# Weight remainders moved from GpSimd to the Vector engine, roundings moved behind the norms, and half of the sums of squares moved ahead

## The reference

```
mod = silu(c) @ w_ada + b_ada                      # six shift/scale/gate vectors
h = modulate(rmsnorm(x)); same for the context
u, q, k, v, z, beta, g = mixer_inputs(h)           # h @ w_in, short convolutions, l2norm of q and k
o = bidirectional gated delta rule, chunks of 64 (here 128 tokens each)
y = concat(fourier(u), rmsnorm(o) * silu(z)) @ w_out
x += gt1 * rmsnorm(y)
x += gt2 * rmsnorm((silu(conv3x3(gate)) * val) @ w_down),  val, gate = modulate(rmsnorm(x)) @ w_up
layer A: x += (bgate * conv3(cgate * h)) @ w_out_a,  bgate, cgate, h = rmsnorm(x) @ w_in_a
layer B: x += (gelu(y) * (rglru forward + backward)(conv4(u))) @ w_out_b,  y, u = rmsnorm(x) @ w_in_b
after A and after B:  x += mixture of 32 experts, top 2 (rmsnorm(x));  x += sigmoid(rmsnorm(x) @ w_ple_gate + b) * (p @ w_ple)
out = rmsnorm(x)
```

## Time and profile before

| | us |
|---|---|
| median of 3 runs (1904.95 to 1909.45) | 1907.88 |
| the profiled execution, its time | 1911.88 |
| its span, first to last instruction | 1910.1 |
| busy: PE / DVE / ACT / POOL | 1692.1 / 717.3 / 506.2 / 452.3 |
| mean granted TensorE clock | 0.944 |

### The profile page before, as it was taken

The page is one execution under the profiler, slowest core; times in us unless marked ns, Lnnn a source line. Parts: engine busy times, 40 slices in busy tenths (PEclk is TensorE's granted clock), DMA queues, the critical chain, the costliest instruction groups (busy, mean ns, idle before and its releaser), DMA issues.

```text
span 1910.1 us, 25856 instructions
## 1 busy us (share of the span) xinstructions
PE 1692.1 (89%) x10638; PEld 1148.1 (60%) x10638; DVE 717.3 (38%) x1312; ACT 506.2 (27%) x772; POOL 452.3 (24%) x211
## 2 busy tenths in 40 slices
PE   5988886999979779999999998894799999999987
PEld 2677686999969744443443446793644444444447
DVE  1447534899257531221221213537412212212223
ACT  3434343444433111111111105346211111111123
POOL 2336324587438210000000004461100000000011
PEclk9999887999989879999999998897899999999999
DMA  9122442343636529999999993332569999999970
GB/s 407 59 108 85 181 188 89 133 177 127 213 118 250 223 100 390 429 428 428 428 428 429 428 428 155 145 132 100 253 254 429 428 428 428 428 429 429 429 296 23
DMA packets 37510, 527.99 MB, mean 276 GB/s; under 512 B 4160, under 2 KB 4288, under 8 KB 4800
## 3 DMA queue, kind: packets, MB, share of 16 engines
q1 hardware_dynamic: 36864, 525.22, 66.7%
q10 hardware_dynamic: 576, 1.75, 0.3%
HBM read 525.91 MB, written 1.05 MB: 276 GB/s over the span
## 4 chain that ended last, share of the span: by engine, by line
PE 51%; DMA 32%; DVE 10%; ACT 5%; issue 1%; POOL 0%; SPq 0%; DVEq 0%; ACTq 0%
DMA ring<-in_w_up 30%; PE bank L469 23%; PE bank L933 14%; PE bank L534 2%; PE bank L959 2%; DMA ring<-in_dense 2%; PE bank L462 2%; ACT ring_rounded L1077 1%; PE bank L889 1%; DVE hT L1595 1%; PE bank L890 1%; PE bank L639 1%; ACT L1107 1%; DVE xn L1582 1%; DVE work L1654 1%
## 5 line engine op out<-in xcount | busy, mean ns | idle before, releaser
L1463 POOL TENSOR_TENSOR ring_rounded<-ring,ring_rounded 128x2048 fp32r<-128x2048 f32 (+1 forms) x81 | 362.0, 4490 | 405.4 <-ACT ring_rounded L1077 405.4
L933 PE MATMUL bank<-ring,work 128*64 128x512 f32 x1536 | 342.6, 600 | 35.5 <-DMA ring<-in_w_up 33.4
L469 PE MATMUL bank<-xn_rounded,ring_rounded 128*128 128x256 f32 (+1 forms) x2560 | 355.6, 292 | 14.3 <-DVE xn_rounded L1569 14.2
L469 PEld LDWEIGHTS bank<-xn_rounded,ring_rounded 128*128 128x128 f32 x2560 | 330.6, 197 | 21.1 <-issue 17.1
L933 PEld LDWEIGHTS bank<-ring,work 128*64 128x64 f32 x1536 | 109.5, 138 | 264.5 <-issue 208.2
L469 PE MATMUL bank<-work_rounded,ring_rounded 128*128 128x256 f32 (+1 forms) x1424 | 221.1, 301 | 46.7 <-POOL work_rounded L1540 26.9
L1533 POOL TENSOR_TENSOR work<-work_rounded,work 128x128 f32<-128x128 f32 x64 | 24.3, 401 | 863.5 <-PE bank L952 854.0
L469 PEld LDWEIGHTS bank<-work_rounded,ring_rounded 128*128 128x128 f32 x1424 | 194.0, 197 | 57.4 <-issue 27.8
L959 PE MATMUL bank<-ring,work 128*64 128x512 f32 x1024 | 226.8, 595 | 0.0
L2018 DVE TENSOR_TENSOR work<-work,bank 128x512 f32<-128x512 f32 x32 | 22.0, 688 | 429.2 <-PE bank L933 429.2
L1077 ACT ACTIVATE ring_rounded<-ring 128x2048 fp32r<-128x2048 f32 (+1 forms) x88 | 154.7, 1808 | 63.8 <-PE bank L469 43.4
(11 more groups left out here) (304 smaller groups left out, 1726.5 us busy)
## 6 DMA issues: line engine op xcount, KB each, us to landing
ring<-in_w_up SPq DMA_DIRECT2D x64, 2048.0 KB, 17.3
ring<-in_w_down SPq DMA_DIRECT2D x64, 2048.0 KB, 13.2
ring<-in_dense SPq DMA_DIRECT2D x50, 2048.0 KB, 8.0
work<-in_w_gate SPq DMA_DIRECT2D x32, 2048.0 KB, 21.8
ring<-in_w_gate SPq DMA_DIRECT2D x32, 2048.0 KB, 21.5
ring<-in_dense SPq DMA_DIRECT2D x8, 1408.0 KB, 6.2
ring<-in_dense SPq DMA_DIRECT2D x2, 1024.0 KB, 14.5
work<-in_ctx SPq DMA_DIRECT2D x1, 1024.0 KB, 6.6
```

Source lines behind the costliest of these rows:

```text
L469: last = mm(out, rv(ring[r][:, at:at + P]), rv(x[part][k]), start=k == 0 and j == 0, stop=k == n_k - 1 and j == 2)
L933: last = mm(b[64 * y:64 * y + 64, :], xg[:, k, 64 * y:64 * y + 64], ws[y][:, 512 * k:512 * k + 512], start=k == 0, stop=k == KT - 1)
L1463: pool.tensor_tensor(rv(w), w, rv(ring[HIGH_SLOT[n]][:, a:b]), ALU.subtract).then_inc(S["w_low"], 1)
```

## The change

1. `BY_DVE` is gone; `by_dve` in `plan` is now a set of (chunk, half). DVE makes both halves of `w_in` chunks 3 and 4, `w_out` 1, `w_up` 1, `w_in_a` 1 to 5, `w_out_a` 0 and 1, `ple0` 1, `w_in_b` 0 to 3, `w_out_b` 0 and 1, `ple1` 1, and the seven halves of before: 45 of 88. It does so in a new helper, `weights_low`, called at set places in its stream.
2. ACT's `split_next` moves: in the front behind the gates' exponential (`w_in` 4); behind the `cat` tiles (`w_out` 1); behind `scaled_input` instead of before the squares (`w_up` 1, `w_in_a` 1); behind the last `yT` tile (`w_out_a` 1); behind the norm of layer B (`w_in_b` 1).
3. `sum_squares` can be called in two parts. In `w_out`, `down`, `out_a` and `out_b` the first four tiles are summed before the projection's last use.
4. In z and u the six sums of squares of q and k come two behind each of the first three uses, none behind the last; ACT copies the second u bank after all six roots.

```diff
-    by_dve = [first["w_down"] + c for c in range(2, 8)] + [first["w_in_a"]]
+    by_dve = [(first[name] + c, half) for name, chunks in (
+        ("w_in", (3, 4)), ("w_out", (1,)), ("w_up", (1,)), ("w_in_a", range(1, 6)), ("w_out_a", range(2)), ("ple0", (1,)),
+        ("w_in_b", range(4)), ("w_out_b", range(2)), ("ple1", (1,))) for c in chunks for half in range(2)]
+    by_dve += [(first["w_down"] + c, 0) for c in range(2, 8)] + [(first["w_in_a"], 0)]
...
             for b in range(2, uses):
+                if summed and b == uses - 1:
+                    sum_squares(early)
                 dense_split(*tiles(b), x)
...
-                    first = {"z": 0, "u": 3}[stage] + 2 * b
-                    for a in range(first, min(first + 2 - b * (stage == "z"), 6)):
+                    for a in {("z", 0): (0, 1), ("z", 1): (2, 3), ("u", 0): (4, 5)}.get((stage, b), ()):
                         sums_qk(a)
...
-        projection("w_out", "w_out", 4, [...], ("cat_ready", 1))
+        projection("w_out", "w_out", 4, [...], ("cat_ready", 1), True)
-        sum_squares()
+        sum_squares(late)
         ready = norm_input()
         projection("up", "w_up", FT, xparts, ready)
         for b in range(4):
+            if b == 3:
+                sum_squares(early)
             dense_split(USE["down"] + b, ...)
...
@scalar
-        split_next()                       # behind the q SiLUs
         act.wait_ge(S["ab_dve"], 1)
...
         signal(act.activation(gtmp[1], gtmp[1], ACT.Exp, scale=-1.0), "ab_act")
+        split_next()
...
-        split_next()                       # behind the roots of o
         for h in range(HEADS):
             act.wait_ge(S["cat_gated"], h + 1)
             high(cath[:, 4 + h], cat[:, 4 + h])
+        split_next()
...
             root(bank[4][:, 0:SEQ], bank[5][:, 0:SEQ], 1.0 / D, "ss_ready", "rstd_ready")
-            split_next()                   # end of rows
...
         scaled_input(24)
+        split_next()
...
         scaled_input()                     # before in_a
+        split_next()
-            if j in (1, 2, 3, 5, 6, 7):
+            if j in (1, 2, 3, 5, 6):
                 split_next()
...
         high(yh[:, 6:8], yT[:, 6:8])
+        split_next()
...
-                if layer == 0 and b % 2:
+                if layer == 0 and b == 1:
                     split_next()
...
         scaled_input()                     # before in_b
+        split_next()
@vector
+        def weights_low(n, halves=(0, 1)):
+            for half in halves:
+                a, b = parts_of(n)[half]
+                dve.wait_ge(S["w_high"], 2 * SPLITS.index(n) + half + 1)
+                w = ring[SLOT[n]][:, a:b]
+                count["w_low_dve"] = count.get("w_low_dve", 0) + 1
+                v.tensor_tensor(rv(w), w, rv(ring[HIGH_SLOT[n]][:, a:b]), ALU.subtract).then_inc(S["w_low_dve"], 1)
...
             free(ins, n)                   # q convolutions, b = 0, 1
+            weights_low(FIRST["w_in"] + 3, (b,))
...
                "gates_ready")
+        weights_low(FIRST["w_in"] + 4)
...
             low(cat[:, 4 + h], cath[:, 4 + h], "cat_ready")
+        weights_low(FIRST["w_out"] + 1)
         residual(lambda k: gains[:, 3, k:k + 1])
         scaled(hT, lambda k: gains[:, 2, k:k + 1])
+        weights_low(FIRST["w_up"] + 1)
...
         scaled(hT, lambda k: par("norm_mix", k, 1))
+        weights_low(FIRST["w_in_a"] + 1)
...
+            if j in (1, 2, 3, 5):
+                weights_low(FIRST["w_in_a"] + (1, 2, 3, 5).index(j) + 2)
+            elif j == 6:
+                weights_low(FIRST["w_out_a"])
         low_pair(6)
+        weights_low(FIRST["w_out_a"] + 1)
...
             scaled(hT, lambda k: par("norm_ple", 8 * layer + k, 1))
+            weights_low(FIRST[f"ple{layer}"] + 1)
...
+                if layer == 0 and b == 1:
+                    weights_low(FIRST["w_in_b"])
...
         scaled(hT, lambda k: par("norm_mix", 8 + k, 1))
+        weights_low(FIRST["w_in_b"] + 1)
...
             free(last, n)                  # conv4 of layer B, uses b = 0..3
+            if b % 2:
+                weights_low(FIRST["w_in_b"] + 2 + b // 2)
+        weights_low(FIRST["w_out_b"])
...
                 last = v.tensor_tensor(gi[d][:, j], gi[d][:, j], uu[:, j], ALU.mult)
+                if d == 0 and j == KT // 2:
+                    weights_low(FIRST["w_out_b"] + 1)
```

More of the change, by code:

```diff
@@ L163, in plan @@
         for half in range(2):
-            name = "w_low_dve" if n in by_dve and half == 0 else "w_low"
+            name = "w_low_dve" if (n, half) in by_dve else "w_low"
             made[name] += 1
             low_done[n, half] = (name, made[name])
-    return first, use, free, slot, arrival, load_after, splits, high_slot, high_after, by_dve, low_done
-FIRST, USE, FREE, SLOT, ARRIVAL, LOAD_AFTER, SPLITS, HIGH_SLOT, HIGH_AFTER, BY_DVE, LOW_DONE = plan()
+    return first, use, free, slot, arrival, load_after, splits, high_slot, high_after, low_done
+FIRST, USE, FREE, SLOT, ARRIVAL, LOAD_AFTER, SPLITS, HIGH_SLOT, HIGH_AFTER, LOW_DONE = plan()
 WORK, WORK_N = layout([
@@ L517, in first_uses, with projection @@
                     assert signal(last, "dense_full") == use + 1
-        def projection(stage, chunk, uses, x, ready):
+        early, late = range(4), range(4, KT)
+        def projection(stage, chunk, uses, x, ready, summed=False):
             def tiles(b):
@@ L525, in projection, with sum_squares @@
             for b in range(2, uses):
+                if summed and b == uses - 1:
+                    sum_squares(early)
                 dense_split(*tiles(b), x)
-        def sum_squares():
-            for k in range(KT):
+        def sum_squares(tiles=range(KT)):
+            for k in tiles:
                 if k % 2 == 0:
@@ L534, in sum_squares @@
                 last = mm(bank[4][:, 0:SEQ], ones, sq1[:, k], start=k == 0, stop=k == KT - 1)
-            signal(last, "ss_ready")
-            count["norms"] = count.get("norms", 0) + 1
+            if tiles[-1] == KT - 1:
+                signal(last, "ss_ready")
+                count["norms"] = count.get("norms", 0) + 1
         n_normed = [1]
@@ L823, in _, with norm_input @@
             signal(mm(bank[6 + x][:], ones, sqo[:, x], start=True, stop=True), "o_ss")
-        projection("w_out", "w_out", 4, [[x[:, k] for k in range(KT)] for x in (cath, cat)], ("cat_ready", 1))
+        projection("w_out", "w_out", 4, [[x[:, k] for k in range(KT)] for x in (cath, cat)], ("cat_ready", 1), True)
         xs = [xnT[:, k] for k in range(KT)]
         xparts = [[x[:, k] for k in range(KT)] for x in (xh, xnT)]
-        def norm_input():
-            sum_squares()
+        def norm_input(tiles=range(KT)):
+            sum_squares(tiles)
             n_normed[0] += 1
             return "xn_ready", KT * (n_normed[0] - 1) + 1
-        sum_squares()
+        sum_squares(late)
         ready = norm_input()
@@ L838, in _ @@
         for b in range(4):
+            if b == 3:
+                sum_squares(early)
             dense_split(USE["down"] + b, [(FIRST["w_down"] + 2 * b + i, 0) for i in range(2)],
                         [[x[:, k] for k in range(FT)] for x in (prodh, prod)], None if b else ("prod_ready", 1), FT, P)
-        sum_squares()
+        sum_squares(late)
         ready = norm_input()
         projection("in_a", "w_in_a", 12, xparts, ready)
-        projection("out_a", "w_out_a", 4, [[x[:, k] for k in range(KT)] for x in (yh, yT)], ("y_ready", 1))
+        projection("out_a", "w_out_a", 4, [[x[:, k] for k in range(KT)] for x in (yh, yT)], ("y_ready", 1), True)
         def moe(layer):
-            ready = norm_input()
+            ready = norm_input(late)
             w_r = par("w_router").rearrange("p (l k c) -> p l k c", l=2, k=KT)
@@ L1021, in _ @@
                     for x, w in enumerate((wr, wi))])
-        projection("out_b", "w_out_b", 4, [[rr[d][:, k] for k in range(KT)] for d in (1, 0)], ("lru_h", 1))
+        projection("out_b", "w_out_b", 4, [[rr[d][:, k] for k in range(KT)] for d in (1, 0)], ("lru_h", 1), True)
         moe(1)
@@ L1864, in _ @@
             low(prod[:, f], prodh[:, f], "prod_ready")
-        for n in BY_DVE:
-            a, b = parts_of(n)[0]
-            dve.wait_ge(S["w_high"], 2 * SPLITS.index(n) + 1)
-            w = ring[SLOT[n]][:, a:b]
-            v.tensor_tensor(rv(w), w, rv(ring[HIGH_SLOT[n]][:, a:b]), ALU.subtract).then_inc(S["w_low_dve"], 1)
+        for c in range(2, 8):
+            weights_low(FIRST["w_down"] + c, (0,))
+        weights_low(FIRST["w_in_a"], (0,))
         residual(lambda k: gains[:, 4, k:k + 1])
```

6 lines of the change are left out of this document (4 added, 2 removed).

## The result

The changed kernel takes 1864.09 us, the median of four runs (1860.25 to 1865.43), against 1907.07 for the kernel before in the same comparison: a ratio of 0.9771 with a 95% interval of 0.9751 to 0.9791. Timed once more, beside later runs, it gave 1864.68 us and 0.9772 [0.9758, 0.9786]. The forecast was 1863.0. The profiled execution took 1865.19 us with a span of 1863.4 and a mean granted clock of 0.957 (0.944 before).

What follows compares the result with a forecast made beforehand. TensorE had half the chain, DMA a third; POOL's remainders, at 0%, were said to stop DVE. Terms 1.4 + 9.5 + 7.2 + 7.2 + 10.0 + 6.8 + 3.3 - 0.5 = 44.9 us off 1907.88 gave 1863.0, range 1852 to 1877.

Steps and rivals of the forecast that it cites:

- Start of `w_out`: Chunk 1's rounding moved behind the `cat` roundings lets `w_out` start earlier and run through: gain 9.5 us, bounds 7.5 to 9.8.
- Norm before `up`: Rounding and POOL's remainders gone from the norm between `w_out` and `up`: gain 7.2 us, from 6.8 to 8.8.
- Norm before `in_a`: Same pattern as before `up`, two blocked additions to `hT`: gain 7.2 us, same bounds.
- the clock comes back too: Rival, 16%: shorter norms keep 2.4 GHz, both residual norms give 8.8 us and 1.6 to 3 more behind each: 1855 us.
- `in_a` and `out_a`: TensorE's 8.78 us wait and slower last products at `out_a` go: 10.8 us, taken as 10.0, bounds 6 to 11.3.
- `ple` to `in_b`: Rounding of `w_in_b` chunk 1 moves behind the norm, sums run at 2.4 GHz: gain 6.8 us, 3.7 if the clock falls.
- `in_b` and the gates: Gates' DVE product no longer stopped, 4.5 us, less 1.2 for chunk 3's late halves: gain 3.3 us, bounds 0 to 4.6.
- Front: From q to the gates: 0.8 + 4.5 us gained, 3.9 lost waiting at `w_in` chunk 3: gain 1.4, bounds -1.5 to +3.5.
- `out_b`: Early sums leave the last pair's way through DVE and ACT less hidden: 0.5 us lost.
- Late remainders: Rival, 17%: the tight places each miss by 2 to 4 us, 12 to 16 us are given back: 1878 us.
- The loop swallows it: Rival, 4%: first expert loop's stream is DMA bound from its prefetch on, all gained before is lost: 1898 us.
- DVE becomes the bound: Rival, 3%: at 6 us a remainder, 8 chunks in `in_a` and `in_b` cost 7.3 us each: 1921 us.

Runs made afterwards that it cites:

- the product: Changed kernel plus two extra 128x2048 fp32 products on GpSimd, on scratch in SBUF, starting with the residual behind `w_out`: 1870.8 us, 0.9802.
- the fill: Changed kernel plus three extra GpSimd fills (memset) of SBUF scratch, starting with the residual behind `w_out`: 1863.3 us, 0.9766.
- the run with the norms alone: Kernel before, with only `w_up` 1 and `w_in_a` 1 rounded behind the scaling and their remainders made by DVE: 1892.7 us, 0.9928.
- `w_in` 3: Changed kernel with both remainder halves of `w_in` chunk 3 made by GpSimd again: 1859.0 us, 0.9740.
- the front as before: Changed kernel with `w_in` 3 and 4 remainders, `w_in` 4 rounding, q and k sums and u copies as in the kernel before: 1863.5 us, 0.9759.
- the places undone: Changed kernel with ACT's roundings back where they stood before, DVE's 45 remainders and the early sums kept: 1877.8 us, 0.9826.
- the run with POOL's remainders in the new places: Changed kernel with its roundings and sums kept, but the 38 new remainders made by GpSimd again: 1880.2 us, 0.9849.

## Why the prediction was right

**The bound and the mechanism.** The long `hT` additions were named as POOL's doing from one coincidence in a timeline. The product and the fill show it, and the run with the norms alone gives the price, 15.3 us for two norms where the forecast had 14.4. Of the signs named ahead, the longest addition (0.419 us), the start of `out_a` (no wait) and DVE's remainders (2.29 us) came out as said; `up` began at 320.3 instead of 318, since the unchanged stages ahead of it took 2.4 us more.

**Start of `w_out`**: 9.5 forecast, 9.5 measured. TensorE's wait, 5.76 us before, is 1.5, and the stream behind it has no stop.

**Norm before `up`**: 7.2 and 7.4. **Norm before `in_a`**: 7.2 and 8.8. The difference is the clock: its 16 sums took 5.13 us, those before `up` 6.58. With it the rival *the clock comes back too* came true in one of two places. The windows over the first four microseconds of `in_a` and of `up` in the changed kernel (window, its length, busy us and instructions of PE, weight loads, DVE, ACT and POOL, then the granted clock, DMA share, GB/s), and of `in_a` before:

```profile
529.40:533.40 4.00, 4.00 (x33) 4.00 (x34) 4.00 (x12) 2.62 (x6) 0.00 (x0) 1.00 0.00 0
320.30:324.30 4.00, 4.00 (x19) 4.00 (x20) 3.52 (x10) 3.56 (x10) 0.00 (x0) 0.50 0.00 0
```

```profile
554.00:558.00 4.00, 3.82 (x21) 3.85 (x22) 4.00 (x12) 2.13 (x6) 0.00 (x0) 0.60 0.00 0
```

`in_a` now starts at the upper level (2.4 GHz), with 33 products in 4 us; `up` still starts at the lower (1.2 GHz), with 19, although the same 3.57 us of idle time stand between the two groups of sums in both norms. It is not luck of one execution, and not the rule either: the first 4 us of `in_a` are at the upper level in six profiles (the changed kernel twice, `w_in` 3, the product, the fill, the front as before), and at a mean of 0.57 to 0.64 in the five others with a shorter norm. Those of `up` are at the upper level throughout in one alone, that with the places undone, where `up` and `down` then took 199.0 us instead of 201.0:

```profile
322.50:326.50 4.00, 4.00 (x31) 3.76 (x31) 3.55 (x10) 3.53 (x10) 0.00 (x0) 1.00 0.00 0
```

**`in_a` and `out_a`**: 10.0 taken, 12.3 measured. The reckoning had given 10.8 and was cut for its margins, which held: TensorE waited for no remainder in `in_a`, and the 1.5 us of slow start that I had put in front of it did not come, because of the clock. The early sums of `out_a`, put at 0.5, cost 0.8.

**`ple` to `in_b`**: 6.8 and 7.7 (6.5 in the changed kernel's second profile), and the clock came back as forecast: the 16 sums took 3.72 us in all ten profiles with the rounding behind the norm and 6.6 in the three with it in front. PE's timeline, and the window over the same sums (at 0.57 before):

```profile
1168.61 3.72 PE L541 MATMUL bank<-xn,consts 128*128 128x256 f32 x16 [1.14 <-ACT xn L1074]
```

```profile
1168.60:1172.40 3.80, 3.72 (x16) 2.96 (x16) 0.40 (x2) 1.55 (x4) 0.00 (x0) 1.00 1.01 431
```

**`in_b` and the gates**: 3.3 and 4.0. The late half of chunk 3 was reckoned ready 38.9 us after the first product, 1.2 late; its end at 1213.2 is 38.1 us after 1175.1, and TensorE waited 0.4. The gates' products ran unbroken, as forecast 27.8 us for 128:

```profile
1223.44 27.79 PE L465 MATMUL bank<-work,ring 128*128 128x256 f32 x128
```

**Front**: 1.4 and 1.5, with the wait of 3.8 us at `w_in` 3 where 3.9 had been worked out. It was right that this edit costs there; it was left as part of the change's price, and taking it out was worth 4 to 5 us in the profiles. **`out_b`**: -0.5 was forecast, and -0.9 to -1.1 measured.

**What the sum left out, and where luck came in.** The delta rule's -3.5 belongs to one execution: thirteen profiles, all with the same instructions there, gave 121.7 to 127.1 us, with the old front (122.7, 122.9, 123.6, 126.3) as with the new. The lengths of the loops (465.7 to 467.9 us from the first expert product to the last) spread in the same way over all of them. In the profiles the changed stages gained 50.1 us (48.7 in the changed kernel's second profile), 4 to 5 more than the 44.9 forecast, above all in `in_a`. The unchanged stages lost 3.3, which leaves the 46.7 of the spans. The medians gained 43.0 and 43.3: the profiled execution before was 4.8 us above its median, the one after 1.1. No view shows where in the kernel those 3.7 us lie. So each stage's mechanism is confirmed, but that the total came within 1.1 us of the forecast is in part luck: terms mis-sized by up to 2.3 us, mostly too low, against losses in stages put at 0.

**Rivals.** *Late remainders* would have shown TensorE waiting in `in_a` or `in_b` for over 3 us: none and 0.4. It came true in the run with POOL's remainders in the new places (5.3), so the margins did hang on the engine. *The loop swallows it*: no, the first loop began 38 us earlier, the second 48, and they took 467.9 and 467.4 us where they had 466.7 and 466.2, within the spread above. *DVE becomes the bound* decided from 5.2 us a half: DVE's took 2.29 at most.

**What stays open.** Why the clock comes back behind one norm and not behind the other; why the routing is 1.0 us shorter only behind early sums, and only half of the time; and what the early sums are worth by the total, which no comparison here can tell from nothing.

## What to carry to other kernels

An engine with a share of 0% in the chain can still hold up the one that has 10%: look for instructions of one line whose longest is ten times the median, and for what runs beside them. Work of GpSimd that reads SBUF is free only where DVE has nothing short and serial to do; either give it to DVE (half the time here, 2.29 against 4.6 us) or move what triggers it out of the norm. Before an edit that does both is kept everywhere, look at each place: here one needed the engine, one the place, most either, and one (`w_in` 3) was better without. And a total that comes out as forecast does not show that its terms did: twice here two misses cancelled.

## What the runs showed of the hardware

- A DVE instruction of 128x16, 0.17 us of work, stands for 2.8 to 4.5 us beside a GpSimd remainder and ends with it (within 0.03 us), whatever its own size. The one of 2.80 has a single tensor operand in SBUF (TENSOR_SCALAR), so it isn't only instructions with two. The Trainium skill (SBUF — State Buffer, "Who interferes with whom") lists `tensor_scalar` among those that can use both ports, under conditions; the row agrees that it can be stopped, and shows no more. The RECIPROCAL behind it, also with one SBUF tensor, began beside the next remainder and was not stopped (0.25 us).
- The reverse is seen as well, and small here: a remainder of POOL that begins while a DVE instruction with two SBUF inputs is running takes longer. In `up`, in the changed kernel, eight remainders of 128x2048 began 0.32 to 0.34 us before such an instruction's end and took 4.81 to 4.82 us; the first of each of those pairs, with a DVE instruction that reads PSUM beside its start, took 4.63 to 4.64. For 128x1408 it is 3.38 to 3.42 us against 3.24 to 3.25, whether the DVE instruction is a remainder or not; beside the last DVE remainder of `down`, begun 0.44 us before its end, 4.89. The prediction had reckoned with such holds, and TensorE waited for a POOL remainder only once in the changed kernel, 0.3 us. GpSimd's times are rough in this profile, but these repeat.
- A GpSimd product of 128x2048 fp32 with one tensor as both inputs took 3.6 us, a remainder of two tensors 4.6.
